# Prompt attention: scaling three heads later, scores two heads ahead

## The chip, the cores and the metric

The kernel runs on one NeuronCore of a Trainium2 chip. The metric is the device time of one launch in microseconds (us), the median of several. Engines are named TensorE (PE, its weight loads PEld), VectorE (DVE), ScalarE (ACT), GpSimd (POOL) and SyncE (SP).

## The reference

Two layers of a hybrid decoder trunk, for a prompt of 512 tokens and eight short samples. Only one part of it matters here, the sparse attention of the prompt, by blocks of 128 queries over at most 512 keys:

```python
def sparse_attention_block(q, iq, iw, keys_k, keys_v, keys_i, q_pos, k_pos, topk):
    ...
    score = jnp.einsum('bqh,bqhl->bql', iw.astype(F32), jax.nn.relu(logits))
    ...
    top_score, idx = lax.top_k(score, topk)
    ...
    s = jnp.einsum('bqgrd,bqkgd->bqgrk', qg, k_sel) * A_HEAD_DIM ** -0.5
    s = jnp.where(valid[:, :, None, None, :], s, MASK_VALUE)
    p = jax.nn.softmax(s, axis=-1)
    o = jnp.einsum('bqgrk,bqkgd->bqgrd', p, v_sel)
```

There are 8 query heads of width 64, 4 key and value heads, and every query keeps 128 keys. The kernel does not gather: it takes all keys up to the block's end and adds a bias that is 0 for a kept key and -1e30 for the others. All arithmetic is float32.

## The kernel before

Five engines run streams of their own, each in the order written, with semaphores between them (`wait_ge`, `then_inc`). The prompt attention is the third block of `stage_a` (L791 to L936). It loops over four query blocks i = 0 to 3 with L = 128 (i + 1) keys, in each of two layers. A block has three parts: eight index products (L820) with their ReLU and sum, a top-k on VectorE (`topk`, nothing of note in block 0), and the **head loop** over eight heads h, numbered n = 8i + h.

In the head loop a head passes these steps:

- TensorE, s(h): scores into bank n % 2, a 64-row product of L columns (L830). It waits until the head two before has been biased.
- VectorE: biased scores into `St` (L927), the negated row maximum into `mx` (L930).
- ScalarE: the exponential into `Pr` with its row sum into `sm` (L889, the row sum read by a second instruction).
- TensorE, t(h): i + 1 transposes into bank 2 + n % 2 (L838).
- ScalarE: copy to `PT` (L896).
- TensorE, v(h): i + 1 products with the values into bank 4 + n % 2 (L849). It waits for that copy and for the scaling of the head two before (`att_out`).
- VectorE: reciprocal of the row sum (L922) and scaling of v(h) into `on` (L935).

Between these, TensorE and ScalarE work off another task, the input projection of the jobs r1, r2 and c2: `Share` spreads 120 of its steps over points by weight. One head has two points, A ahead of t(h) and B behind it. A step is either a full one, F (L360, a 512-column product), or a strip step, S (L357, four small ones side by side). ScalarE takes a finished projection tile at the same points (L435). By the weights, the steps at (A, B) of heads 0 to 8 (head 8 is the last turn of the loop, with v(7) alone) are:

```
block 0: (F,-) (F,F) (-,F) (F,-) (F,F) (-,F) (F,-) (F,-) (F,F)
block 1: (S,-) (S,S) (-,S) (S,-) (F,F) (-,F) (F,-) (F,-) (F,F)
block 2: (-,F) (F,-) (F,S) (-,S) (S,-) (S,-) (S,S) (-,S) (S,-)
block 3: (F,-) (F,F) (-,F) (S,-) (S,S) (-,S) (S,-) (S,S) (-,S)
```

TensorE's order in turn h is s(h+1), A, t(h), B, v(h-1), with s(0) ahead of the loop. VectorE's in turn h is reciprocal of h-2, biasing and maximum of h, scaling of h-2. ScalarE's is exponential of h, A, copy of h-1, B. After the loop TensorE waits for all scalings and transposes `on` (L867).

Of the kernel before, what the change touches and what calls it, by code (L numbers as in the profile page):

```python
# [7 lines left out]
ALU = mybir.AluOpType  # L8
# [124 lines left out]
def trunk(nc, inp, out):  # L133

    es = ExitStack()
    with es:
# [49 lines left out]
        ps = [es.enter_context(nc.psum_tensor(f"ps{i}", [P, 512], F32)) for i in range(8)]  # L186
# [473 lines left out]
        def stage_a(l):  # L660
# [134 lines left out]
            St, Pr = ar.take(2, 512), ar.take(2, 512)  # L795
            PT = ar.take(2, 512)
            on = ar.take(2, 512)
            mx, sm = ar.take(2, 8), ar.take(2, 8)
            weights = []
            for i in range(NT):  # L800
                weights += [1] * 8 + [(1, 18, 25, 34)[i]] + [1] * 18
# [1 line left out]
            with nc.Block() as block:  # L803
# [4 lines left out]
                @block.tensor  # L808
                def _(pe):
                    for i in range(NT):  # L810
                        L = (i + 1) * P
                        q0 = i * P
                        for h in range(8):
                            n = i * 8 + h
                            r = (h % 2) * 64
                            if n >= 2:
                                pe.wait_ge(S("idx_relu"), n - 1)
                            if h < 2 and i:
                                pe.wait_ge(S("att_biased"), 8 * i)
                            pe.matmul(ps[n % 2][:, 0:L], iqT[r:r + 64, h // 2, q0:q0 + P], ikT[r:r + 64, 0:L]).then_inc(S("idx_logits"), 1)  # L820
                            share.point("pe", pe)

                        def scores(h):
                            n = i * 8 + h
                            r = (h % 2) * 64
                            if h < 2:
                                pe.wait_ge(S("idx_relu"), 8 * i + 8)
                            if n >= 2:
                                pe.wait_ge(S("att_biased"), n - 1)
                            pe.matmul(ps[n % 2][:, 0:L], qT[r:r + 64, h // 2, q0:q0 + P], k2T[r:r + 64, h // 2, 0:L]).then_inc(S("att_scores"), 1)  # L830

                        def turn_probs(h):
                            n = i * 8 + h
                            if n >= 2:
                                pe.wait_ge(S("probT_taken"), n - 1)
                            pe.wait_ge(S("att_probs"), n + 1)
                            for s in range(i + 1):
                                mm = pe.transpose(ps[2 + n % 2][:, s * P:s * P + P], Pr[:, n % 2, s * P:s * P + P], ident)  # L838
                            mm.then_inc(S("probT_ready"), 1)

                        def values(h):
                            n = i * 8 + h
                            pe.wait_ge(S("probT_taken"), n + 1)
                            if n >= 2:
                                pe.wait_ge(S("att_out"), n - 1)
                            if h == 1 and i:
                                pe.wait_ge(S("att_turn_taken"), i)
                            for s in range(i + 1):
                                mm = pe.matmul(ps[4 + n % 2][:, h * 64:h * 64 + 64], PT[:, n % 2, s * P:s * P + P],  # L849
                                               vn[:, s, (h // 2) * 64:(h // 2) * 64 + 64], start=(s == 0), stop=(s == i))  # L850
                            mm.then_inc(S("att_values"), 1)
                        share.point("pe", pe)
                        scores(0)
                        for h in range(9):
                            if h < 7:
                                scores(h + 1)
                            share.point("pe", pe)
                            if h < 8:
                                turn_probs(h)
                            share.point("pe", pe)  # L860
                            if h >= 1:
                                values(h - 1)
                        pe.wait_ge(S("att_out"), 8 * i + 8)
                        if i >= 1:
                            pe.wait_ge(S("att_turn_taken"), i)
                        for c in range(4):
                            mm = pe.transpose(ps[5][:, c * P:c * P + P], on[:, i % 2, c * P:c * P + P], ident)  # L867
                        mm.then_inc(S("att_turned"), 1)
                    share.end("pe", pe)

                @block.scalar
                def _(act):
                    for i in range(NT):
                        L = (i + 1) * P
                        for h in range(8):
                            n = i * 8 + h
                            act.wait_ge(S("idx_logits"), n + 1)
                            if n >= 2:
                                act.wait_ge(S("idx_summed"), n - 1)
                            act.activation(R[:, n % 2, 0:L], ps[n % 2][:, 0:L], ACT.Relu, scale=0.125).then_inc(S("idx_relu"), 1)  # L880
                            share.point("act", act)
                        share.point("act", act)
                        for h in range(9):
                            n = i * 8 + h
                            if h < 8:
                                act.wait_ge(S("att_max"), n + 1)
                                if n >= 2:
                                    act.wait_ge(S("probT_ready"), n - 1)
                                act.activation(Pr[:, n % 2, 0:L], St[:, n % 2, 0:L], ACT.Exp, bias=mx[:, n % 2, 0:1],  # L889
                                               accum_out=sm[:, n % 2, 0:1]).then_inc(S("att_probs"), 1)  # L890
                            share.point("act", act)
                            if h >= 1:
                                act.wait_ge(S("probT_ready"), n)
                                if n >= 3:
                                    act.wait_ge(S("att_values"), n - 2)
                                act.activation(PT[:, (n - 1) % 2, 0:L], ps[2 + (n - 1) % 2][:, 0:L], ACT.Copy).then_inc(S("probT_taken"), 1)  # L896
                            share.point("act", act)
                        act.wait_ge(S("att_turned"), i + 1)
                        act.activation(brT[:, 0:4, i * P:i * P + P], ps[5][:, :].rearrange("p (c t) -> p c t", c=4), ACT.Copy).then_inc(S("att_turn_taken"), 1)
                    share.end("act", act)  # L900

                @block.vector
                def _(dve):
                    for i in range(NT):
# [10 lines left out]
                        vch.link(dve, dve.tensor_tensor(score[:, L - P:L], score[:, L - P:L], K("neg"), ALU.add))  # L915
                        topk(dve, score[:, 0:L], work[:, 0:L], bias[:, 0:L], m8, TOPK_P if L > TOPK_P else L)
                        vch.link(dve, dve.tensor_tensor(bias[:, L - P:L], bias[:, L - P:L], K("neg"), ALU.add))
                        for h in range(10):
                            n = i * 8 + h
                            if h >= 2:  # L920
                                dve.wait_ge(S("att_probs"), n - 1)
                                vch.link(dve, dve.reciprocal(sm[:, n % 2, 1:2], sm[:, n % 2, 0:1]))  # L922
                            if h < 8:
                                dve.wait_ge(S("att_scores"), n + 1)
                                if n >= 2:
                                    dve.wait_ge(S("att_probs"), n - 1)
                                dve.scalar_tensor_tensor(St[:, n % 2, 0:L], ps[n % 2][:, 0:L], 0.125, bias[:, 0:L],  # L927
                                                         ALU.mult, ALU.add).then_inc(S("att_biased"), 1)
                                dve.wait_ge(S("att_biased"), n + 1)
                                dve.tensor_reduce(mx[:, n % 2, 0:1], St[:, n % 2, 0:L], AX, ALU.max, negate=True).then_inc(S("att_max"), 1)  # L930
                            if h >= 2:
                                dve.wait_ge(S("att_values"), n - 1)
                                if h == 2 and i >= 2:
                                    dve.wait_ge(S("att_turned"), i - 1)
                                dve.tensor_scalar(on[:, i % 2, (h - 2) * 64:(h - 2) * 64 + 64], ps[4 + n % 2][:, (h - 2) * 64:(h - 2) * 64 + 64],  # L935
                                                  sm[:, n % 2, 1:2], None, ALU.mult).then_inc(S("att_out"), 1)  # L936
            stage_a_sample(l, idx_at, keep, vn, kTs, iwn, qT, ikT, iqT)

        def topk(dve, score, work, bias, m8, k):
# [1695 lines left out]
```

## Time and profile before

| | us |
|---|---|
| median of 3 runs | 3984.4 (3983.34 to 3989.88) |
| the profiled execution | 3989.57 |
| its span, first to last instruction | 3987.7 |
| TensorE busy in it | 3528.7 |
| VectorE busy in it | 1734.9 |
| ScalarE busy in it | 728.2 |

The span is one execution as the profiler saw it; the execution's own time lies 1.9 us above it. Busy time of TensorE comes from pipelined products whose ends are modelled. A line of the timeline gives the start in us from the span's start, the duration, engine, line of the kernel, operation, what it writes and reads with the shape, the number of instructions merged, and in brackets the idle time of the engine ahead of it and what ended that. A row by stage gives the stretch, its length, busy time (and instructions) of each engine, the granted clock of TensorE as a share of full speed, the share of the DMA engines and GB/s.

### The profile page before, as it was taken

Reading aid. Unit: us, or ns where it says so; the run is one execution under the profiler, and the core shown is the slowest. Engines: PE = TensorE matmul, PEld = TensorE weight load, DVE = VectorE, ACT = ScalarE, POOL = GpSimd, SP = SyncE. Lnnn points to the kernel's source line nnn. Section 1 sums busy time; section 2 is a strip of 40 time slices with the busy share of each in tenths; the row PEclk is TensorE's granted clock in tenths of the full one; section 3 lists DMA queues with packets and bytes.
Section 4 is the critical chain, followed back from the end, with each engine's and each line's share of the span. In section 5 each row is a group of like instructions: output and inputs, shape, how many; then the busy total and the mean of one; then the engine's idle time right before and its main releaser. Section 6 shows DMA issues by size and latency. Waiting matters only on the chain. (4 is left out here: it accounts for less than half of the span.)

```text
span 3987.7 us, 45143 instructions
## 1 busy us (share of the span) xinstructions
PE 3528.7 (88%) x18090; PEld 2452.6 (62%) x18090; DVE 1734.9 (44%) x3249; ACT 728.2 (18%) x1556; POOL 241.9 (6%) x250
## 2 busy tenths in 40 slices
PE   5988899988987878999988888998989886989998
PEld 2543455576666656888845434555756664768887
DVE  2136286133544433555512563940435454144543
ACT  1122222111322200010002222221213221010100
POOL 0000321200010000000000004112000000000000
PEclk9988899888998989999989889998989997999999
DMA  3211255532314022222222114446232221212221
GB/s 116 84 59 39 78 190 173 173 96 91 106 39 126 28 66 75 79 74 70 85 91 85 43 36 151 157 142 205 83 101 75 94 65 50 75 60 85 85 73 66
DMA packets 274202, 365.83 MB, mean 92 GB/s; under 512 B 39006, under 2 KB 170462, under 8 KB 273860
## 3 DMA queue, kind: packets, MB, share of 16 engines
q1 hardware_dynamic: 231580, 260.59, 19.9%
q0 software_dynamic: 21504, 75.51, 5.9%
q10 hardware_dynamic: 20904, 26.78, 1.9%
q8 instruction: 146, 2.39, 0.3%
q14 instruction: 68, 0.56, 0.0%
HBM read 312.50 MB, written 50.34 MB: 91 GB/s over the span
## 5 line engine op out<-in xcount | busy, mean ns | idle before, releaser
L368 PE MATMUL ps<-hT,ring 128*128 128x272 f32 x3072 | 784.4, 410 | 107.9 <-PEq L154 54.8
L368 PEld LDWEIGHTS ps<-hT,ring 128*128 128x128 f32 x3072 | 593.2, 198 | 259.7 <-issue 76.2
L360 PE MATMUL ps<-ring,hT 128*128 128x512 f32 (+3 forms) x1600 | 667.8, 559 | 46.4 <-ACT stage L435 19.0
L360 PEld LDWEIGHTS ps<-ring,hT 128*128 128x128 f32 (+1 forms) x1600 | 283.3, 201 | 343.9 <-issue 306.4
L368 PE MATMUL ps<-branchT,ring 128*128 128x272 f32 x1024 | 283.7, 432 | 75.7 <-DVE arena L478 38.4
L368 PEld LDWEIGHTS ps<-branchT,ring 128*128 128x128 f32 x1024 | 206.9, 208 | 146.8 <-DVE arena L478 45.8
L2450 PE MATMUL ps<-hT,ring 128*128 128x272 f32 x1136 | 279.3, 396 | 17.4 <-DVE hT L623 17.4
L2450 PEld LDWEIGHTS ps<-hT,ring 128*128 128x128 f32 x1136 | 218.0, 192 | 63.6 <-issue 18.2
L947 DVE MAX8 branchT<-arena 32x8 f32<-32x2080 f32 x64 | 148.2, 2316 | 2.2
L948 DVE MATCH_REPLACE8 arena<-branchT,arena 32x2080 f32<-32x2080 f32 x64 | 147.0, 2296 | 0.0
L2450 PE MATMUL ps<-arena,ring 128*128 128x272 f32 x528 | 126.4, 393 | 2.5 <-DMA ring<-in_w_down 2.5
L368 PE MATMUL ps<-arena,ring 128*128 128x272 f32 x512 | 117.8, 393 | 2.2 <-issue 2.2
L2450 PEld LDWEIGHTS ps<-arena,ring 128*128 128x128 f32 x528 | 100.2, 190 | 23.9 <-DMA ring<-in_w_down 3.4
L368 PEld LDWEIGHTS ps<-arena,ring 128*128 128x128 f32 x512 | 97.1, 190 | 22.9 <-issue 3.0
L2450 PE MATMUL ps<-branchT,arena 128*128 128x272 f32 x448 | 111.2, 392 | 0.0
L2450 PE MATMUL ps<-branchT,ring 128*128 128x272 f32 x448 | 111.2, 392 | 0.0
L1186 ACT ACTIVATE branchT<-ps 128x512 f32<-128x512 f32 x128 | 69.5, 594 | 191.4 <-PE ps L1091 191.0
L2450 PEld LDWEIGHTS ps<-branchT,ring 128*128 128x128 f32 x448 | 85.1, 190 | 17.5
L2450 PEld LDWEIGHTS ps<-branchT,arena 128*128 128x128 f32 x448 | 85.1, 190 | 17.5
L2463 ACT ACTIVATE arena<-ps 128x272 f32<-128x272 f32 x60 | 23.8, 397 | 393.3 <-PE ps L2450 393.3
L719 DVE TENSOR_TENSOR branchT<-arena 128x2560 f32<-128x2560 f32 (+1 forms) x4 | 8.6, 2154 | 190.7 <-PEq L679 190.7
L2450 PE MATMUL ps<-branchT,stage 128*128 128x272 f32 x352 | 87.9, 392 | 0.0
(466 smaller groups left out, 4444.6 us busy)
## 6 DMA issues: line engine op xcount, KB each, us to landing
ring<-in_w_in SPq DMA_DIRECT2D x44, 2048.0 KB
ring<-in_w_gu SPq DMA_DIRECT2D x44, 1024.0 KB
spill<-stage ACTq DMA_DIRECT2D x72, 256.0 KB
arena<-spill SPq DMA_DIRECT2D x16, 1024.0 KB, 5.6
ring<-in_w_branch SPq DMA_DIRECT2D x16, 1024.0 KB
ring<-in_w_down SPq DMA_DIRECT2D x8, 1536.0 KB
ring<-in_w_down SPq DMA_DIRECT2D x8, 1280.0 KB
ring<-in_w_out SPq DMA_DIRECT2D x4, 2048.0 KB
```

Source lines behind the costliest of these rows:

```text
L360: mm = pe.matmul(bank[0:m, 0:w], hT[:, c, t0:t0 + m], slot3(j)[:, c, 0:w], start=(c == 0), stop=(c == kn - 1))
L368: mm = pe.matmul(bank[:, 0:HALF], slot3(j)[:, c, at:at + P], src, start=(c == 0), stop=(c == kn - 1))
L719: vch.link(dve, dve.tensor_tensor(t2, a2, a2, ALU.mult))
L947: vch.link(dve, dve.max(m, src))
L948: vch.link(dve, dve.match_replace(work, m, src, TAKEN))
L1186: act.activation(KT[:, bb, j, :], ps[j][:, :], ACT.Copy).then_inc(S("kt_ready"), 1)
L2450: mm = pe.matmul(bank(n, p), left[:, c, :], r[:, c, :], start=(c == 0), stop=(c == k - 1))
L2463: act.activation(part_of[n % 2][0], bank(n, 1), ACT.Copy).then_inc(S("p1_copied"), 1)
```

## The change

VectorE scales the result of head h-3 in turn h instead of that of h-2, and does so after the biasing and the maximum of head h, reciprocal included; its loop has eleven turns in place of ten. The row sums get four columns in place of two, so that a sum outlives the later scaling. TensorE makes s(0) and s(1) ahead of the loop and s(h+2) in turn h, behind t(h) and ahead of B. Its order in a turn becomes A, t(h), s(h+2), B, v(h-1). ScalarE's order stays.

```diff
@@ -795,7 +795,7 @@
             St, Pr = ar.take(2, 512), ar.take(2, 512)
             PT = ar.take(2, 512)
             on = ar.take(2, 512)
-            mx, sm = ar.take(2, 8), ar.take(2, 8)
+            mx, sm = ar.take(2, 8), ar.take(4, 2)
             weights = []
             for i in range(NT):
                 weights += [1] * 8 + [(1, 18, 25, 34)[i]] + [1] * 18
@@ -851,12 +851,13 @@
                             mm.then_inc(S("att_values"), 1)
                         share.point("pe", pe)
                         scores(0)
+                        scores(1)
                         for h in range(9):
-                            if h < 7:
-                                scores(h + 1)
                             share.point("pe", pe)
                             if h < 8:
                                 turn_probs(h)
+                            if h < 6:
+                                scores(h + 2)
                             share.point("pe", pe)
                             if h >= 1:
                                 values(h - 1)
@@ -887,7 +888,7 @@
                                 if n >= 2:
                                     act.wait_ge(S("probT_ready"), n - 1)
                                 act.activation(Pr[:, n % 2, 0:L], St[:, n % 2, 0:L], ACT.Exp, bias=mx[:, n % 2, 0:1],
-                                               accum_out=sm[:, n % 2, 0:1]).then_inc(S("att_probs"), 1)
+                                               accum_out=sm[:, n % 4, 0:1]).then_inc(S("att_probs"), 1)
                             share.point("act", act)
                             if h >= 1:
                                 act.wait_ge(S("probT_ready"), n)
@@ -915,11 +916,8 @@
                         vch.link(dve, dve.tensor_tensor(score[:, L - P:L], score[:, L - P:L], K("neg"), ALU.add))
                         topk(dve, score[:, 0:L], work[:, 0:L], bias[:, 0:L], m8, TOPK_P if L > TOPK_P else L)
                         vch.link(dve, dve.tensor_tensor(bias[:, L - P:L], bias[:, L - P:L], K("neg"), ALU.add))
-                        for h in range(10):
+                        for h in range(11):
                             n = i * 8 + h
-                            if h >= 2:
-                                dve.wait_ge(S("att_probs"), n - 1)
-                                vch.link(dve, dve.reciprocal(sm[:, n % 2, 1:2], sm[:, n % 2, 0:1]))
                             if h < 8:
                                 dve.wait_ge(S("att_scores"), n + 1)
                                 if n >= 2:
@@ -928,12 +926,16 @@
                                                          ALU.mult, ALU.add).then_inc(S("att_biased"), 1)
                                 dve.wait_ge(S("att_biased"), n + 1)
                                 dve.tensor_reduce(mx[:, n % 2, 0:1], St[:, n % 2, 0:L], AX, ALU.max, negate=True).then_inc(S("att_max"), 1)
-                            if h >= 2:
-                                dve.wait_ge(S("att_values"), n - 1)
-                                if h == 2 and i >= 2:
+                            if h >= 3:
+
+                                u, hu = n - 3, h - 3
+                                dve.wait_ge(S("att_probs"), u + 1)
+                                vch.link(dve, dve.reciprocal(sm[:, u % 4, 1:2], sm[:, u % 4, 0:1]))
+                                dve.wait_ge(S("att_values"), u + 1)
+                                if hu == 0 and i >= 2:
                                     dve.wait_ge(S("att_turned"), i - 1)
-                                dve.tensor_scalar(on[:, i % 2, (h - 2) * 64:(h - 2) * 64 + 64], ps[4 + n % 2][:, (h - 2) * 64:(h - 2) * 64 + 64],
-                                                  sm[:, n % 2, 1:2], None, ALU.mult).then_inc(S("att_out"), 1)
+                                dve.tensor_scalar(on[:, i % 2, hu * 64:hu * 64 + 64], ps[4 + u % 2][:, hu * 64:hu * 64 + 64],
+                                                  sm[:, u % 4, 1:2], None, ALU.mult).then_inc(S("att_out"), 1)
             stage_a_sample(l, idx_at, keep, vn, kTs, iwn, qT, ikT, iqT)
 
         def topk(dve, score, work, bias, m8, k):
```

## Rows read from the trace of the kernel before

**Rows 1.** Busy table of the page: engine, busy us, share of span, instructions.
```profile
PE 3528.7 (88%) x18090; PEld 2452.6 (62%) x18090; DVE 1734.9 (44%) x3249; ACT 728.2 (18%) x1556; POOL 241.9 (6%) x250
```

**Rows 2.** Stages: four head loops of layer 0, block 2 of layer 1.
```profile
core 0: us, PE busy (x) PEld busy (x) DVE busy (x) ACT busy (x) POOL busy (x), PEclk, DMA share, GB/s
231.50:249.00 17.50, 16.74 (x62) 9.05 (x60) 7.74 (x33) 6.20 (x25) 0.00 (x0) 1.00 0.04 15
...
275.30:303.00 27.70, 25.53 (x107) 14.44 (x108) 9.61 (x33) 7.83 (x25) 0.00 (x0) 0.66 0.25 86
...
335.70:362.30 26.60, 23.94 (x154) 14.09 (x154) 11.65 (x33) 9.50 (x25) 0.00 (x0) 0.82 0.03 11
...
406.00:437.40 31.40, 28.15 (x179) 17.17 (x179) 13.75 (x32) 11.27 (x25) 0.00 (x0) 0.83 0.04 11
...
2302.10:2326.90 24.80, 22.17 (x155) 13.07 (x155) 11.62 (x32) 9.38 (x25) 0.00 (x0) 0.88 0.03 12
```

**Rows 3.** Waits of TensorE, then VectorE, whole span: total us, times, longest.
```profile
PE ps L838 <- ACT arena L889: 51.7, 10, 9.4
...
PE ps L867 <- DVE arena L935: 3.6, 8, 0.5
...
DVE arena L935 <- PE ps L849: 76.7, 64, 4.4
```

**Rows 4.** Timeline, TensorE, block 3: start, us, engine, line, operation, idle before.
```profile
433.53 0.63 PE L838 MATMUL ps<-cst,arena 128*128 128x128 f32 x4 [0.36 <-ACT arena L889]
```

**Rows 5.** Timeline, TensorE, block 3 at full clock.
```profile
420.66 1.12 PE L830 MATMUL ps<-arena 64*128 64x512 f32 x2
421.71 0.42 PE L357 MATMUL ps<-ring,hT 128*32 128x128 f32 x8
...
423.49 1.12 PE L830 MATMUL ps<-arena 64*128 64x512 f32 x2
...
426.88 1.12 PE L830 MATMUL ps<-arena 64*128 64x512 f32 x2
427.93 0.66 PE L838 MATMUL ps<-cst,arena 128*128 128x128 f32 x4
...
429.91 1.12 PE L830 MATMUL ps<-arena 64*128 64x512 f32 x2
```

**Rows 6.** Timeline, ScalarE, block 3: last instruction of head 5's exponential.
```profile
426.78 0.18 ACT L889 ACTIVATION_READ_ACCUMULATOR arena<-arena 128x1 f32 x1
```

**Rows 7.** Timeline, TensorE, block 0.
```profile
233.03 0.33 PE L838 MATMUL ps<-cst,arena 128*128 128x128 f32 x1 [0.37 <-ACT arena L889]
233.29 0.48 PE L830 MATMUL ps<-arena 64*128 64x128 f32 x2
...
236.48 1.02 PE L360 MATMUL ps<-ring,hT 128*128 128x512 f32 x2
237.34 0.33 PE L849 MATMUL ps<-arena 128*128 128x64 f32 x2
237.60 0.48 PE L830 MATMUL ps<-arena 64*128 64x128 f32 x2
238.01 1.12 PE L360 MATMUL ps<-ring,hT 128*128 128x512 f32 x2
238.97 0.27 PE L838 MATMUL ps<-cst,arena 128*128 128x128 f32 x1
239.09 0.33 PE L849 MATMUL ps<-arena 128*128 128x64 f32 x2
239.35 0.48 PE L830 MATMUL ps<-arena 64*128 64x128 f32 x2
...
245.15 0.33 PE L849 MATMUL ps<-arena 128*128 128x64 f32 x2
245.31 1.08 PE L360 MATMUL ps<-ring,hT 128*128 128x512 f32 x2
```

**Rows 8.** Stages: block 1 of layer 0, its later heads; columns as rows 2.
```profile
295.00:300.00 5.00, 5.00 (x26) 3.07 (x24) 2.31 (x8) 1.84 (x7) 0.00 (x0) 1.00 0.02 6
```

## The prediction

> **What bounds the kernel now.** I read the busy table first: TensorE is busy 88% of the span, VectorE 44% [rows 1]. That is a mean over stages, and the change touches one: the head loops of the prompt attention, four query blocks in each of two layers. So next the table by stage, one stretch per head loop [rows 2]: 17.5, 27.7, 26.6 and 31.4 us in layer 0, 103.2 us in all; the one row of layer 1 that stands there (block 2) is 24.8 us. In layer 0 TensorE is busy 16.74 + 25.53 + 23.94 + 28.15 = 94.4 of 103.2 us, VectorE 7.74 + 9.61 + 11.65 + 13.75 = 42.8 us. That leaves 8.8 us of TensorE idle in a layer, some 17.6 us in both, as all that any order of these instructions could win without making TensorE itself faster.
>
> Then the waits [rows 3], where a reader can go wrong. VectorE's scaling of a head's result (L935) waits for TensorE all 64 times, 76.7 us in all: that looks like the thing the change takes away. The two rows of TensorE tell the other half. In the whole launch its transposes of probabilities (L838) waited for ScalarE 10 times and its last transposes (L867) for VectorE 8 times; scores (L830), values (L849) and projection steps inside the head loops have no such row. Eight of the ten are the first transpose of each loop, after top-k, and two are the seventh in block 3, 0.36 us [rows 4]. So VectorE waits because TensorE is late, not the other way round.
>
> The timeline of block 3 shows it [rows 5]. I write s for a score product, t for a head's transposes, v for its value products, S for a strip step (L357) and F for a full step (L360) of the projection. From s at 420.66: S at 421.71, then t and v, and the next s at 423.49, with no idle time noted before any of them. And t of head 5 at 427.93 does not wait for its exponential: ScalarE's last instruction for it began at 426.78 and took 0.18, so it was ready at 426.96, 0.97 us early [rows 5, 6]. **The loop is bound by TensorE's own stream**, and the chain through VectorE and ScalarE has slack.
>
> **The change part by part.** *The order of TensorE.* Before: s(h+1), A, t(h), B, v(h-1), where A and B are the two share points of a head, each with zero or one projection step. After: A, t(h), s(h+2), B, v(h-1), with s(0), s(1) in front, as now in effect. The instructions are the same; only who follows whom differs, and that can be priced. From block 0, start to start [rows 7]: s 0.41 (237.60 to 238.01), F 0.96, t 0.12, v 0.26 (239.09 to 239.35): a head of 1.75 us. v followed by F instead of s takes 0.16 (245.15 to 245.31), and t followed by s 0.26 (233.03 to 233.29) against 0.12 followed by v. So s costs about 0.1 us more to enter than a 128-row product, whichever stands before it. The change has one entry and one exit of s per head, as now. New pairs are t to s (seen: 0.26, of which 0.12 is the t itself), s to v (not seen; s took 0.41 to F) and v to t (not seen; between 0.16 before F and 0.26 before s). I take 0.41 and 0.16, since v and t are 128-row products like F. The bound for both is 0.1 us a head to either side, times 64 heads: 6.4 us down or up.
>
> *Strips.* Block 3, only A holding a strip: 420.66 to 423.49, 2.83 us a head; only B holding one: 426.88 to 429.91, 3.03 us [rows 5]. A strip next to a score shares its change-over; one elsewhere pays, half of those 0.2 us each on entering, I take 0.1. The change moves the score from ahead of A to ahead of B, so A strips begin to pay and B strips stop. By the list of A and B steps ahead: in blocks 2 and 3 three A strips stand behind a score now and two B strips will; in block 1 three and three. Net one strip more in two blocks of two layers: 4 x 0.1 = 0.4 us slower.
>
> *Waits.* The 0.36 us of t(7) in block 3 goes, since s(7) will be issued a head earlier: 2 x 0.36 = 0.7 us faster. What is late next there is TensorE itself.
>
> *VectorE.* Nothing is added but an empty turn of its loop; a reciprocal and a scaling move behind the reduction of a later head. Queued behind the scaling's wait for v(h-3) is the next head's biasing, which waits for s(h+1), and that stands behind v(h-3) on TensorE: nothing new is late. On TensorE, v(h-1) waits for the scaling of h-3, which now comes after the maximum of h. The exponential and t(h) wait for that same maximum and stand ahead of v(h-1), so they cover it. Without cover it would be one scaling, 0.28 us a head; the four columns of sums are what lets it lag. I take 0; the bound is one such scaling at the end of each of the eight loops, 2.2 us slower, and nothing faster. ScalarE's order is untouched, and so are the DMA queues: no transfer is moved past anything.
>
> *The ends of a loop.* First: top-k, biasing, maximum, exponential, t(0), as now. Last: v(7), scaling, L867, as now.
>
> Sum: 0.4 - 0.7 = **-0.3 us**. The profiled execution took 3989.57 us (span 3987.7 and 1.9 outside), 5.2 us above the median of the runs shown, 3984.4, so -0.3 on the median is 3984.1; I give 3984.
>
> **The clock** is the larger unknown. Block 1 has a mean granted clock of 0.66, and TensorE is back at full speed by 295 [rows 2, 8]; block 2 took 26.6 us in layer 0 and 24.8 us in layer 1 with the same work, at 0.82 and 0.88 [rows 2]. So 1.8 us a block moves with where the clock comes back, and a new order moves it. Eight blocks partly cancelling: I take four the same way, 7 us either way.
>
> **The rivals.** *Hidden waits, faster.* The busy time of a pipelined engine may hide gaps. The mark for it would be s: at 512 columns 1.05 us to the next (420.66 to 421.71) [rows 5], while F of the same 512 columns took 0.86 (236.48 to 237.34) [rows 7]. If those 0.2 us were a wait for data that the new order satisfies early, it would win 64 x 0.2 = 13 us, 3971. Against it: s costs its 0.41 at 128 columns ahead of F, and F waits for no result of the head loop. The Trainium skill, Perfetto Trace Analysis, Identifying the Most-Contended Engine, speaks for this rival: matmul busy share is called a poor measure of TensorE's limit, and the share of weight loads a better one. Here weight loads fill 17.17 of 31.4 us in block 3, 55% [rows 2], so by that rule TensorE would have room, and the time would be that of this rival; the start-to-start times contradict it. Chance 0.06.
>
> *The clock returns later in block 1, slower.* Its heads from 295 to 303, 8 us, run at full speed now. At half speed they would take 8 us longer in each layer, 16 us, 4000. What could do it: after the change a score stands between the two full steps that block 1 meets in its fifth head, where now they are split by a transpose alone. It decides from about 4 us of delay a layer, 8 in both. Against it: block 2, which also starts low, is back early in both layers [rows 2]. Chance 0.04.
>
> *The change does not do what it says.* TensorE takes its instructions in order, so the new order takes place; if VectorE's lag is never used, the time is that of the forecast. It has no chance of its own.
>
> **How the numbers follow.** Forecast 0.90, hidden waits 0.06, late clock 0.04. 0.2%, 8 us, is about what a measurement can tell from no change; the forecast's spread of 7 us lies inside it, so faster 0.06, same 0.90, slower 0.04. The range is 3984 less and plus 7 (the unseen pairs 6.4, the clock 7, seldom both at their ends): 3977 to 3991. It leaves both rivals out, 0.10.
>
> **What would show it.** Right: the head loops last as long as now to within 2 us each; TensorE has no idle row inside them, and the 0.36 us wait is gone; VectorE's waits at its scaling fall or move to its biasing; s costs the same ahead of B and v. Wrong: heads of block 3 under 2.7 us in the full-clock part (hidden waits), a mean clock in block 1 well under 0.6 (late clock), or v in a wait for VectorE.

## The result

The changed kernel took 3995.86 us (median of 16 runs), the kernel before 3984.26 us beside it: 1.0027 times, 95% interval 1.0019 to 1.0035. It is 11 us slower, where 3984 us (3977 to 3991) and no measurable change were forecast. (A ratio is taken over all runs and is not the quotient of two medians.) Measured once more it was 3996.0 against 3985.66, 1.0018 (1.0005 to 1.0031).

The changed kernel's profiled execution took 3994.99 us, 5.4 us more than that of the kernel before. Its head loops, stage by stage, as in [rows 2] (columns as there):

```profile
231.80:249.30 17.50, 16.68 (x60) 8.52 (x59) 7.36 (x32) 6.56 (x25) 0.00 (x0) 1.00 0.04 15
275.60:302.20 26.60, 24.49 (x106) 13.48 (x106) 9.49 (x32) 8.25 (x25) 0.00 (x0) 0.68 0.26 89
335.10:361.20 26.10, 23.62 (x155) 13.58 (x155) 11.62 (x32) 9.73 (x25) 0.00 (x0) 0.84 0.03 11
406.40:436.70 30.30, 27.37 (x179) 16.41 (x179) 13.79 (x33) 11.51 (x25) 0.00 (x0) 0.85 0.04 11
...
2302.20:2327.80 25.60, 23.08 (x155) 13.37 (x155) 11.62 (x33) 9.73 (x25) 0.00 (x0) 0.85 0.03 12
```

In layer 0 they sum to 100.5 us against 103.2, so this stretch alone would say that the change gained. Block 2 of layer 1 is 25.6 us where it was 24.8. The mean granted clock in a block is what moved with each length: 0.68, 0.84 and 0.85 in blocks 1 to 3 of layer 0 against 0.66, 0.82 and 0.83. All five loops lie within the 2 us that the prediction gave as the sign of being right, so that sign could not show what happened.

The waits, which answer [rows 3]:

```profile
PE ps L838 <- ACT arena L890: 51.0, 8, 9.4
...
DVE arena L925 <- PE ps L830: 70.5, 48, 4.0
...
DVE arena L937 <- PE ps L849: 42.9, 44, 2.0
```

TensorE now waits for the exponential 8 times instead of 10: the two waits of [rows 4] are gone. VectorE's wait at the scaling fell from 76.7 to 42.9 us and turned up at the biasing (L925), 70.5 us. And the stream of TensorE in block 3 at full clock, which answers [rows 5]:

```profile
425.31 1.12 PE L830 MATMUL ps<-arena 64*128 64x512 f32 x2
426.37 0.42 PE L357 MATMUL ps<-ring,hT 128*32 128x128 f32 x8
426.72 1.10 PE L849 MATMUL ps<-arena 128*128 128x64 f32 x8
427.66 0.61 PE L838 MATMUL ps<-cst,arena 128*128 128x128 f32 x4
428.20 1.12 PE L830 MATMUL ps<-arena 64*128 64x512 f32 x2
```

s, S, v, t and the next s: 2.89 us for a head with a strip behind its score, where A with a strip took 2.83 before. So far everything is as forecast, and the time is not.

**Where the time went.** Layer 1 shows it, because it starts the same way in both kernels, with 12.2 and 12.3 us of index products in block 0. Four stretches of the kernel before, from the first transpose of block 1 to its end, block 3's index products and top-k, block 3's loop, and the whole stage of the layer:

```profile
2243.60:2269.20 25.60, 25.13 (x106) 14.09 (x106) 8.09 (x29) 7.24 (x23) 0.00 (x0) 0.68 0.27 93
...
2327.50:2371.30 43.80, 35.35 (x79) 12.90 (x78) 32.94 (x64) 7.82 (x15) 0.00 (x0) 0.90 0.18 66
2371.30:2400.20 28.90, 28.03 (x179) 17.04 (x179) 11.49 (x29) 10.45 (x23) 0.00 (x0) 0.86 0.04 12
2187.40:2400.20 212.80, 183.00 (x765) 88.83 (x765) 121.63 (x320) 53.56 (x144) 0.00 (x0) 0.87 0.13 45
```

The same four of the changed kernel:

```profile
2242.10:2269.20 27.10, 26.58 (x106) 14.47 (x106) 8.03 (x29) 7.72 (x24) 0.00 (x0) 0.63 0.25 88
...
2328.20:2375.10 46.90, 38.55 (x81) 13.54 (x78) 32.85 (x64) 7.80 (x15) 0.00 (x0) 0.85 0.17 62
2375.10:2402.70 27.60, 27.19 (x178) 16.27 (x178) 11.44 (x29) 10.71 (x24) 0.00 (x0) 0.89 0.04 11
2185.60:2402.70 217.10, 187.83 (x764) 89.17 (x764) 121.29 (x320) 54.92 (x144) 0.00 (x0) 0.87 0.13 44
```

The stage is 4.3 us longer: 1.5 in block 1, 3.1 in the index products and top-k of block 3, -1.3 in block 3's loop, the rest in blocks 0 and 2. TensorE is busy nearly all of these loops, so multiply the length of a loop by its mean clock, and the difference is gone: block 1 25.6 x 0.68 = 17.4 against 27.1 x 0.63 = 17.1, block 3 28.9 x 0.86 = 24.9 against 27.6 x 0.89 = 24.6. TensorE's work did not grow; it was done at the lower of the two clock levels (1.2 and 2.4 GHz) for longer.

How the clock came back in block 1 of layer 1 can be read off the durations. The kernel before (a full step at half clock takes about 2 us, at full clock 1.0 to 1.1):

```profile
2255.88 2.07 PE L360 MATMUL ps<-ring,hT 128*128 128x512 f32 x2
2257.75 0.64 PE L838 MATMUL ps<-cst,arena 128*128 128x128 f32 x2
2258.17 1.91 PE L360 MATMUL ps<-ring,hT 128*128 128x512 f32 x2
2259.88 0.68 PE L849 MATMUL ps<-arena 128*128 128x64 f32 x4
2260.49 0.70 PE L830 MATMUL ps<-arena 64*128 64x256 f32 x2
```

Two full steps with one transpose stage between them, and by the score at 2260.49 (0.70 us) the clock is up. The changed kernel:

```profile
2254.51 2.02 PE L360 MATMUL ps<-ring,hT 128*128 128x512 f32 x2
2256.33 0.63 PE L838 MATMUL ps<-cst,arena 128*128 128x128 f32 x2
2256.89 1.22 PE L830 MATMUL ps<-arena 64*128 64x256 f32 x2
2258.04 2.08 PE L360 MATMUL ps<-ring,hT 128*128 128x512 f32 x2
2259.91 0.95 PE L849 MATMUL ps<-arena 128*128 128x64 f32 x4
2260.65 0.63 PE L838 MATMUL ps<-cst,arena 128*128 128x128 f32 x2
2261.22 1.02 PE L830 MATMUL ps<-arena 64*128 64x256 f32 x2
2262.17 1.12 PE L360 MATMUL ps<-ring,hT 128*128 128x512 f32 x2
```

The score (2256.89, 1.22 us) now stands between the two full steps. The second one ends still at half clock, the values and the transposes after it run at half clock too, and the clock is up only at the full step of 2262.17.

Block 3's index products meet the clock at another place too. In the changed kernel:

```profile
2332.74 2.07 PE L820 MATMUL ps<-arena 64*128 64x512 f32 x2
2334.73 2.07 PE L360 MATMUL ps<-ring,hT 128*128 128x512 f32 x2
```

a product and a full step at 2 us each; in the kernel before only the first steps are slow:

```profile
2332.03 2.07 PE L360 MATMUL ps<-ring,hT 128*128 128x512 f32 x2
...
2335.66 1.12 PE L360 MATMUL ps<-ring,hT 128*128 128x512 f32 x2
```

Top-k cannot start before these products are done, so this shows in full: 46.9 us against 43.8. That the late clock of block 1 brought this about is not shown; "The place in time" below comes back to it.

### The profile page after: what moved, and what is told of

It reads as the page before. It is cut to its first block and busy times, and to the rows that moved or that the text cites. A ratio compares the mean times of both kernels' runs of the same rounds, so it can differ in the third digit from the quotient of the medians.

```text
span 3993.1 us, 45187 instructions
## 1 busy us (share of the span) xinstructions
PE 3538.2 (89%) x18090; PEld 2456.3 (62%) x18090; DVE 1734.1 (43%) x3249; ACT 731.2 (18%) x1556; POOL 244.5 (6%) x250
## 5 line engine op out<-in xcount | busy, mean ns | idle before, releaser
L2452 PE MATMUL ps<-hT,ring 128*128 128x272 f32 x1136 | 279.3, 396 | 17.4 <-DVE hT L623 17.4
L2452 PEld LDWEIGHTS ps<-hT,ring 128*128 128x128 f32 x1136 | 218.0, 192 | 63.7 <-issue 18.2
L2452 PEld LDWEIGHTS ps<-arena,ring 128*128 128x128 f32 x528 | 100.2, 190 | 24.5 <-DMA ring<-in_w_down 4.0
```

The source lines that it names most:

```text
L2452: mm = pe.matmul(bank(n, p), left[:, c, :], r[:, c, :], start=(c == 0), stop=(c == k - 1))
```

## The experiments

Ratios are to the kernel before, measured beside each. "Old" and "new" are TensorE's orders s(h+1), A, t(h), B, v(h-1) and A, t(h), s(h+2), B, v(h-1).

**One half of the change at a time.** TensorE's order alone:

```diff
                         scores(0)
+                        scores(1)
                         for h in range(9):
-                            if h < 7:
-                                scores(h + 1)
...
+                            if h < 6:
+                                scores(h + 2)
```

> TensorE's new order alone (scores two heads ahead); VectorE keeps the old order, scaling two heads later and ahead of nothing new. Theory tail (the heads at the end of a loop are left without a 512-column score, TensorE's clock falls there and the next block's index products run at half speed): all of the loss, +8 to +14 us over the kernel before. Theory VectorE (the later scaling costs): 0 +-3 us. Theory phase (any shift of a microsecond moves where the clock comes back, in either direction): anything within +-10 us, with no reason to equal the changed kernel.

Measured: 3995.31 us, 1.0011 (0.9993 to 1.0029). Three of its runs took 3973 to 3976 us and eight 3991 to 4003, so one kernel has launches 20 us apart (a twelfth took 7177 us and is not in the ratio); it says little by itself.

VectorE's order alone, with TensorE's lines as before:

```diff
-                        for h in range(10):
+                        for h in range(11):
...
-                                vch.link(dve, dve.reciprocal(sm[:, n % 2, 1:2], sm[:, n % 2, 0:1]))
...
+                            if h >= 3:
...
+                                u, hu = n - 3, h - 3
```

> VectorE's new order alone (scaling three heads later, behind the next maximum); TensorE keeps the old order. Theory tail: 0 +-3 us against the kernel before. Theory VectorE: +8 to +14 us. Theory phase: TensorE's stream is bound by itself, so it starts each product when it did and the phase stays too, 0 +-3 us.

Measured: 3984.01 us, 0.9996 (0.9985 to 1.0007). The later scaling costs nothing. Its profile, 3979.45 us, has 212.7 us for the stage in layer 1, as the kernel before.

**Which product of the order.** My first theory was that the heads at a loop's end, left without a score, let the clock fall. The kernel before with s(7) alone moved ahead:

```diff
-                            if h < 7:
+                            if h < 6:
                                 scores(h + 1)
...
+                            if h == 5:
+                                scores(7)
```

> The kernel before with one product moved: the scores of head 7 come one place earlier, behind the transposes of head 5, and the heads at the end of the loop have none ahead of them, as in the changed kernel. Theory tail: most of the loss, +6 to +14 us. Theory phase: within +-10 us and no reason to equal the changed kernel. Theory that the order in the middle of the loop costs: 0 +-3 us.

Measured: 3985.71 us, 0.9999 (0.9989 to 1.0010). And the changed kernel with s(7) put back to its old place:

```diff
+                            if h == 6:
+                                scores(7)
                             share.point("pe", pe)
...
-                            if h < 6:
+                            if h < 5:
                                 scores(h + 2)
```

> The changed kernel with one product put back: scores are made two heads ahead up to head 6, those of head 7 stand at their old place ahead of A in turn 6. Theory tail: the loss goes, 0 +-4 us against the kernel before. Theory that the order in the middle of the loop costs: the loss stays, +8 to +14 us. Theory phase: within +-10 us.

Measured: 3992.17 us, 1.0015 (1.0004 to 1.0026). Both speak against that theory: most of the loss is not in the end of the loop, though held_tail's interval leaves room for a part. In held_tail block 1 of layer 1 took 27.0 us, as in the changed kernel, in tail_only 25.5.

**Which block.** The new order in block 1 alone, with VectorE's new order:

```diff
+                        new = i == 1
                         scores(0)
-                        scores(1)
+                        if new:
+                            scores(1)
                         for h in range(9):
+                            if not new and h < 7:
+                                scores(h + 1)
...
-                            if h < 6:
+                            if new and h < 6:
```

> VectorE's order of the changed kernel, TensorE's new order in block 1 alone, the old one in blocks 0, 2 and 3. Theory late clock (in block 1 a score now stands between the two full steps that bring the clock back, so it comes back later): +6 to +12 us over the kernel before, block 1 of layer 1 some 1.4 us longer (27.0 against 25.6) and what follows meets the clock at another place. Theory phase without that (it is the place of blocks 2 and 3 that counts): within +-4 us.

Measured: 4001.28 us, 1.0027 (1.0015 to 1.0040): as much as the whole change loses, from one block. Its block 1 in layers 0 and 1:

```profile
276.60:305.60 29.00, 28.56 (x106) 15.39 (x106) 7.89 (x28) 7.64 (x23) 0.00 (x0) 0.59 0.24 82
2246.50:2275.30 28.80, 28.36 (x106) 15.32 (x106) 7.89 (x28) 7.64 (x23) 0.00 (x0) 0.60 0.24 82
```

29.0 and 28.8 us at a mean clock of 0.59 and 0.60, where the kernel before had 25.9 and 25.6. The size is more than I had named (27.0). The complement, the old order in block 1 and the new one elsewhere, is the same with one line changed:

```diff
-                        new = i == 1
+                        new = i != 1
```

> The changed kernel with TensorE's old order in block 1 alone. Theory late clock: the loss goes, 0 +-4 us against the kernel before, block 1 of layer 1 again 25.6 us. Theory phase through blocks 2 and 3: +6 to +12 us, as the changed kernel.

Measured: 3990.65 us, 1.0015 (1.0003 to 1.0027), so the loss did not go altogether. Its block 1 is as before (25.7 and 25.4 us). But block 3 has the same pattern, two full steps in turn 1, and there the clock now came back later in both layers:

```profile
2367.90:2398.20 30.30, 29.85 (x179) 17.61 (x179) 11.27 (x29) 10.68 (x23) 0.00 (x0) 0.81 0.04 11
408.50:438.90 30.40, 29.95 (x180) 17.72 (x180) 11.24 (x29) 10.68 (x23) 0.00 (x0) 0.81 0.04 12
```

30.3 and 30.4 us at 0.81, against 28.9 at 0.86 above. The losses of the two halves, 0.27% and 0.15%, add up to more than that of the whole.

Block 1 over all profiles, from its first transpose to L867, in us:

| profile | order in block 1 | layer 0 | layer 1 |
|---|---|---|---|
| before, before_again | old | 25.9, 25.9 | 25.6, 25.5 |
| dve_only | old | 25.5 | 25.6 |
| tail_only | old | 25.1 | 25.5 |
| block1_old | old | 25.7 | 25.4 |
| pad_before | old | 25.0 | 25.5 |
| after, after_again | new | 24.9, 29.0 | 27.1, 27.0 |
| pe_only | new | 24.9 | 27.1 |
| held_tail | new | 27.4 | 27.0 |
| block1_new | new | 29.0 | 28.8 |
| pad_after | new | 24.9 | 30.4 |

The old order always took 25.0 to 25.9 us, the new one 24.9 to 30.4: 25.5 and 27.3 on the mean, 1.8 us a layer. With the old order the clock came back with the first pair of full steps, whatever the rest of the launch did; with the new order only in three of twelve, all in layer 0.

**The place in time.** Eight more transposes ahead of block 3's index products (about 0.9 us a layer, no part of the result):

```diff
                         mm.then_inc(S("att_turned"), 1)
+                        if i == 2:
+                            for _ in range(8):
+                                pe.transpose(ps[2][:, 0:P], ident, ident)
```

In the changed kernel:

> The changed kernel with eight more transposes into a free bank (about 0.9 us of TensorE a layer, no part of the result) at the end of block 2, ahead of block 3's index products. If work alone counts: +1.8 us over the changed kernel. Theory phase: in the profiles so far the clock falls 1.8 us into block 3's index products in the changed kernel, and they and top-k take 46.9 us, and 4.3 us into them in the kernel before, where they take 43.8; 0.9 us later the fall no longer comes at 1.8, the 46.9 becomes 43 to 44, and the kernel is 2 to 4 us faster than the changed kernel although it does more.

Measured: 3993.21 us, 1.0026 (1.0007 to 1.0044). Block 3's index products and top-k took 42.3 and 43.9 us in place of 47.1 and 46.9, as expected, but block 1 of layer 1 took 30.4 us in place of 27.1, and the sum did not move beyond the interval. In the kernel before:

> The kernel before with the same eight transposes (no part of the result). If work alone counts: +1.8 us over the kernel before. Theory phase: the fall of the clock moves from 4.3 to 3.4 us into block 3's index products, the 43.8 us become 45 to 46.5, and the kernel is 4 to 7 us slower than the kernel before.

Measured: 3981.58 us, 0.9986 (0.9974 to 0.9998): faster with more work, where I had expected slower. Block 3's index products and top-k, layers 1 and 0:

```profile
2318.30:2360.60 42.30, 33.92 (x80) 12.52 (x78) 32.88 (x64) 7.23 (x14) 0.00 (x0) 0.95 0.17 64
...
360.90:403.20 42.30, 33.96 (x81) 12.54 (x79) 32.83 (x64) 7.21 (x15) 0.00 (x0) 0.96 0.17 64
```

42.3 us in both, against 43.8 and 45.5 in the kernel before. The eight transposes, which keep TensorE at work between the loop and the index products, went with a clock that did not fall there at all, so the loss of 3 us at this place can go without touching the order. But the transposes are not what it takes. pe_only, with the new order and no transposes, had the same in layer 1:

```profile
2329.30:2371.60 42.30, 33.78 (x80) 12.56 (x80) 33.06 (x64) 7.82 (x15) 0.00 (x0) 0.96 0.18 68
```

And pad_after with them took 43.9 us in layer 1. Nor does this stretch go by the order: without the transposes it took 43.8 to 46.9 us in profiles with the old order in block 3 (46.9 in layer 0 of tail_only, 45.5 twice in block1_new, whose block 1 was late in both layers) and 42.3 to 47.1 with the new one. So the 3.1 us above can't be put down to the new order, nor to the late clock of block 1; what decides here stays open.

**The same lead, without a score between full steps.** The changed kernel with s(h+2) behind B: A, t(h), B, s(h+2), v(h-1).

```diff
                             if h < 8:
                                 turn_probs(h)
+                            share.point("pe", pe)
                             if h < 6:
                                 scores(h + 2)
-                            share.point("pe", pe)
```

> The changed kernel with the score two heads ahead moved behind B: A, t(h), B, s(h+2), v(h-1). Two full steps of one turn have a transpose alone between them again. Theory late clock: the loss goes, 0 +-4 us against the kernel before, and block 1 goes back to full speed by 42.5 to 44.5 us after its first index product, as in every profile of the old order, where the new order took up to 53.9. Theory that making scores two heads ahead costs by itself: the loss stays, +8 to +14 us.

Measured: 3989.96 us, 1.0009 (0.9997 to 1.0021), no difference that can be measured. The whole stage, block 1's loop and block 3's index products and top-k, in layer 1:

```profile
2186.40:2399.10 212.70, 183.41 (x764) 86.60 (x764) 121.48 (x320) 54.07 (x144) 0.00 (x0) 0.88 0.13 45
2242.90:2268.40 25.50, 25.07 (x106) 13.29 (x106) 7.91 (x29) 7.49 (x23) 0.00 (x0) 0.68 0.27 93
2326.60:2370.50 43.90, 35.38 (x80) 12.97 (x79) 33.03 (x64) 7.82 (x15) 0.00 (x0) 0.94 0.18 66
```

212.7, 25.5 and 43.9 us: the kernel before had 212.8, 25.6 and 43.8. Block 1 of layer 0 took 25.0 us. Scores are made two heads ahead here as well and the scaling is three heads later, so in block 1 neither is what costs; the place of the score between A and B is. For the launch it is weaker: the mean of its runs is 3990.6 us beside 3995.7 for the changed kernel, but the two intervals overlap, and in layer 0 the stage (218.8 us) tells it neither from the changed kernel (218.9) nor from the kernel before (219.8).

The changed kernel again:

> The changed kernel once more, for a second profile and beside the others on one chip. Theory late clock: +8 to +14 us over the kernel before; in blocks 1 or 3 of at least one layer the clock comes back a window later than in any profile of the old order. Theory that the first measurement was chance: 0 +-4 us.

Measured: 1.0018 (1.0005 to 1.0031), as said above. Block 1 of layer 0, and the stage in layer 1:

```profile
277.30:306.30 29.00, 28.53 (x106) 15.39 (x106) 7.95 (x29) 7.65 (x23) 0.00 (x0) 0.59 0.24 82
...
2184.00:2401.20 217.20, 187.81 (x764) 89.15 (x764) 121.47 (x320) 54.92 (x144) 0.00 (x0) 0.87 0.12 44
```

29.0 us at 0.59 in block 1, and in layer 1 217.2 us, as the first profile's 217.1. The kernel before again, one launch:

> The kernel before once more, for a second profile. Theory late clock: its block 1 is back at full speed 42.5 to 44.5 us after the first index product in both layers, and its block 3 at most 8.7 us after its first transpose.

Measured: 3989.53 us; block 1 took 25.9 and 25.5 us (in the table), block 3's loop 29.0 and 28.8 us, the stage of layer 1 212.8 us again.

**The steps themselves.** If full steps in a loop bring the clock back, the share's weights matter more than the order. First the weights of top-k raised, so that some 30 steps leave the head loops and the index products:

```diff
-                weights += [1] * 8 + [(1, 18, 25, 34)[i]] + [1] * 18
+                weights += [1] * 8 + [(1, 68, 71, 82)[i]] + [1] * 18
```

> The kernel before with other weights in the share: some 30 of the 120 projection steps go from the head loops and the index products into top-k, where TensorE sat idle for 9.4, 8.5 and 7.3 us ahead of the first transposes of blocks 1 to 3. If the head loops are bound by TensorE's own stream, every full step moved takes 0.86 us off them and the idle time takes it in: 25 us a layer at most where the clock stays up, -20 to -50 us in all. If the loops are bound by the chain through VectorE and ScalarE: 0 to -5 us.

Measured: 4010.95 us, 1.0064 (1.0042 to 1.0086), the opposite of what I had expected. Blocks 2 and 3 of layer 0, from the first transpose:

```profile
322.70:352.60 29.90, 29.46 (x132) 18.59 (x132) 9.66 (x29) 8.06 (x22) 0.00 (x0) 0.51 0.06 19
398.20:436.30 38.10, 37.65 (x157) 23.90 (x157) 11.41 (x29) 9.66 (x22) 0.00 (x0) 0.51 0.03 6
```

Less work and more time: 29.9 and 38.1 us where the kernel before took 24.5 and 29.0. TensorE is busy 29.46 of 29.9 us and still has a mean clock of 0.51. Of the projection steps these loops held strips alone, and the clock stayed low to their end; block 1, which kept five full steps, took 16.2 and 20.2 us. With the changed kernel's order:

> The changed kernel with the same weights. With few steps left in the head loops TensorE no longer fills them, and the waits that the change loosens are on the path: 3 to 12 us faster than the same weights with the old order. If TensorE binds the loops still: the changed kernel's loss or nothing, 0 to +14 us against the same weights with the old order.

Measured: 4024.69 us, 1.0087 (1.0067 to 1.0107). The looser order gained nothing here either: it took 13.7 us more than the same weights with the old order. Block 1 of layer 1, old order (fill_before) and then new (fill_after):

```profile
2234.20:2254.40 20.20, 19.67 (x87) 12.14 (x87) 7.88 (x29) 6.95 (x23) 0.00 (x0) 0.75 0.33 118
2254.80:2279.90 25.10, 24.62 (x86) 14.06 (x86) 7.94 (x29) 7.48 (x23) 0.00 (x0) 0.59 0.27 95
```

The clock came back later with the new order here too; in layer 0 the loop took 23.4 us where it took 16.2 at full clock with the old order. But a score stands between the first two full steps of block 1 here with the old order as well, and in layer 1 the clock was back at the second of them: the score between two full steps can't be the whole of the cause.

Then the steps set by hand in the other way: the strips of blocks 1 and 2 into their top-k, and four full steps at the start of every loop from block 1 on (the numbers are steps at a point, the last list of a pair the points of a loop):

```diff
+            ones8 = [1, 0, 1, 1, 0, 1, 0, 1]
+            for top, turns in ((1, [1, 0, 1, 1, 0, 1, 1, 0, 1, 1, 0, 1, 1, 0, 1, 0, 1, 1]),
+                               (17, [1, 1, 1, 1, 0, 0, 1, 0, 0, 0, 1, 0, 0, 0, 1, 0, 0, 0]),
+                               (28, [1, 1, 1, 1, 0, 0, 0, 0, 1, 0, 0, 0, 0, 0, 0, 0, 0, 0]),
+                               (18, [1, 1, 1, 1, 1, 0, 1, 0, 1, 0, 1, 0, 1, 0, 1, 0, 1, 1])):
+                weights += ones8 + [top] + turns
```

> The kernel before with the projection steps set by hand: the strips of block 1 go into top-k of block 1, those of block 2 into top-k of block 2, and every head loop begins with four full steps. Theory late clock (full steps early in a loop bring the clock back): block 1 takes 18 to 21 us in place of 25.6, back at full speed 4 to 8 us after its first transpose instead of 16.5; block 2 some 2 us less; block 3 as before; -10 to -25 us in all. If the place of the full steps does not matter: 0 to -6 us, from the idle time filled alone.

Measured: 3973.23 us, 0.9966 (0.9952 to 0.9979), the best of all with the next one. Blocks 1 and 2 and the stage in layer 1:

```profile
2233.40:2252.90 19.50, 18.98 (x73) 10.63 (x71) 7.55 (x27) 6.10 (x20) 0.00 (x0) 0.82 0.00 1
...
2290.60:2310.50 19.90, 18.30 (x94) 11.88 (x92) 9.24 (x27) 7.48 (x20) 0.00 (x0) 0.97 0.03 12
...
2173.90:2380.10 206.20, 174.92 (x764) 87.00 (x764) 121.21 (x320) 53.18 (x144) 0.00 (x0) 0.90 0.13 46
```

Block 1 takes 19.5 us at 0.82 in place of 25.6 at 0.68, and block 2 19.9 at 0.97 in place of 22.8; the stage 206.2 in place of 212.8. Not all of that is the clock: the strips left these loops (block 1's length times clock is 16.0, where it was 17.4), and the index products and top-k ahead of them got longer by what they took in, 29.7 us against 27.4 in block 1 and 37.0 against 34.3 in block 2. Both parts together, block 1 gained 3.7 us, block 2 0.1 and block 3 3.6, and block 0 lost 0.8. With the changed kernel's order:

> The changed kernel with the same steps. Theory late clock: every loop now begins with two turns of two full steps, which the new order splits by a score, so it is 4 to 16 us slower than the same steps with the old order, the clock coming back a window later in some blocks. If the new order costs for a reason that the steps do not touch: +11 us over it, as now. If neither: 0 +-4 us.

Measured: 3972.10 us, 0.9967 (0.9954 to 0.9980).

```profile
2231.00:2249.20 18.20, 17.67 (x74) 10.05 (x72) 7.89 (x28) 6.45 (x20) 0.00 (x0) 0.88 0.00 1
2286.80:2308.60 21.80, 21.04 (x94) 12.45 (x92) 9.50 (x28) 7.83 (x20) 0.00 (x0) 0.85 0.02 9
```

Here I was wrong: the order costs nothing that can be measured on these steps; block 1 is even shorter (18.2 us), block 2 longer (21.8). In turn 0 there are no values, so in the new order B of turn 0 and A of turn 1 are two full steps side by side, while the old order has s(2) between them. That this is why block 1 is shorter was not tested: block 2 begins with the same four full steps and is longer. Whether the new order costs depends on where the full steps lie, not on the order as such.

## Why the prediction was wrong

**Right: the bound and the sum of work.** TensorE's own stream binds the loops, the waits of VectorE were not on the path, the 0.36 us went, and a head costs what the pairs gave: 2.89 us against 2.83 and 3.03. Length times clock agrees to 0.3 us in blocks 1 and 3. The rival of hidden waits fell: no loop became shorter in work. Weight loads filled 16.41 of 30.3 us in block 3 after the change, 54%. By the Trainium skill (Perfetto Trace Analysis, Identifying the Most-Contended Engine) the share of weight loads is one of two measures to judge TensorE's room by; the room that 54% points to is not one that the new order found.

**Wrong: the step on the clock.** I had read from block 2 (26.6 and 24.8 us with the same work) that where the clock comes back moves by 1.8 us a block, and let it fall to either side alike, 7 us, so that the sum held nothing for it. It does not fall to either side alike. In block 1 the old order's spread over all profiles is 25.0 to 25.9 us; the new order gained at most 0.1 on that, three times with 24.9, and took 27.0 to 30.4 the other nine times. That is 1.8 us a layer where the sum had 0.

**Wrong: the rival's size and chance.** The late clock was named with its cause, the score between the two full steps of block 1's fifth head, and was given 0.04. The argument against it, that block 2 starts low and is back early, was no argument: block 2 has a full step in each of turns 0 and 1 with the old order, and its strips come later, while block 1 begins with strips alone. The price was wrong too. I took 8 us a layer, all of the loop at half speed; it was 1.5 in layer 1 and 1.8 a layer over the table. The time came near the 4000 us that the rival gave, but not in the way that it was worked out; that is luck. More was lost where I had not searched, and it is not shown to follow from the order: block 3's index products, 3.1 us in layer 1. Block 3's own pair of full steps cost some 1.4 us a layer in block1_old and nothing in the changed kernel's first profile.

**Open.** The stage sums to 432.6 and 432.7 us over both layers in the two profiles of the kernel before and to 436.0 and 441.9 in those of the changed one, 6 us on the mean of the 10 to 12 between the medians. These four launches themselves lie only 4.6 us apart on the mean, as both profiled launches of the kernel before took 3989.5 us, 4 to 5 above its medians. Block 1 is 3.6 us of the loss over two layers. Layer 0 depends on the launch: block 0's index products, ahead of all that was changed there, took 12.3 to 15.4 us up to the first transpose in profiles of the old order. The rest lies in differences that two profiles of each can't separate from that; I did not trace them. Why the score's place moves the return of the clock is open as well: strips_new and the two kernels with other weights do not fit the two full steps alone.

## What to carry to other kernels

Before moving a product past another on a saturated TensorE, look up where the granted clock is low and which products stand there as it comes back: there, the order of the same work can cost time (1.8 us a layer in block 1 here), and idle time and busy shares do not show it. Where TensorE fills a stage, multiply the stage's length by its mean clock first; if the products agree, search for no wait. And where fill work is spread through a loop, try its large products at the loop's start and its small ones in the idle time ahead of it: the two together were worth 0.34% here.

## What the runs showed of the hardware

A busy TensorE did not by itself get the full clock: with strips, transposes, values and scores alone, it was busy 37.65 of 38.1 us (99%) and had a mean clock of 0.51 (fill_before, block 3 of layer 0). With a score between two full steps, after strips, the clock came back later: in block 1 of layer 1 it came 20.1 us after the first transpose (2262.2 less 2242.1) in place of 16.9 (2260.5 less 2243.6). It is not so everywhere: block 2 has a score between its first two full steps in the old order, and none in the new one, and is 22.8 and 23.5 us from its first transpose on. And more work went with less time: with eight more transposes, 0.9 us a layer, the kernel before took 0.9986 (0.9974 to 0.9998), an interval that ends just short of no change, seen once.
